# A low part's neighbour and a moved wait: two reorderings in a two-block fp32 layer on one core

## The reference, cut to what matters

```python
# first block
mod = silu(c) @ w_ada + b_ada          # 6 x 1024: shift, scale and gate, twice
h = rmsnorm(x) * (1 + sc_m) + sh_m
q, k, v, f, u = split(h @ w_in)        # 8 heads of 64, forget gates, 512 pooling columns
x = x + gt_m * (concat(attention(q, k, v, f), pool(u)) @ w_out)
h = rmsnorm(x) * (1 + sc_f) + sh_f
x = x + gt_f * moe(h)                  # 32 SwiGLU experts, top 2 of the best group of 8
# second block
x = x + hybrid(rmsnorm(x) @ w_in_2)    # stick-breaking attention and a gated recurrence
hn = rmsnorm(x)
x = x + square(relu(hn @ w_ff1)) @ w_ff2   # 1024 -> 4096 -> 1024
out = rmsnorm(x)
```

## Time and profile before

| | |
|---|---|
| median of 3 runs | 787.43 us |
| the profiled execution | 789.42 us |
| its span, first to last instruction | 787.6 us |
| mean granted clock of TensorE | 0.959 |
| PE busy | 705.3 us (90%) |
| DVE busy | 355.1 us (45%) |
| ACT busy | 301.4 us (38%) |
| DMA | 210.24 MB, mean 267 GB/s |

### The profile page before, as it was taken

The page is one execution under the profiler, slowest core; times in us unless marked ns, Lnnn a source line. Parts: engine busy times, 40 slices in busy tenths (PEclk is TensorE's granted clock), DMA queues, the critical chain, the costliest instruction groups (busy, mean ns, idle before and its releaser), DMA issues.

```text
span 787.6 us, 12575 instructions
## 1 busy us (share of the span) xinstructions
PE 705.3 (90%) x5226; PEld 543.6 (69%) x5226; DVE 355.1 (45%) x563; ACT 301.4 (38%) x444; POOL 46.5 (6%) x84
## 2 busy tenths in 40 slices
PE   4999899989876686667999999999998999999996
PEld 3787557964332232222898989898977999999995
DVE  2567742251101000102876677536575555555543
ACT  4344341042110110003676354678355534545432
POOL 0000000000000000000046650000000000000000
PEclk9999997999998887889999999999999999999999
DMA  8999599979999999999874523415344355544101
GB/s 337 413 416 363 216 377 406 421 287 423 420 424 422 424 421 424 420 419 415 317 263 157 209 109 114 167 42 214 107 155 175 126 214 214 214 167 166 43 1 53
DMA packets 33036, 210.24 MB, mean 267 GB/s; under 512 B 4688, under 2 KB 5072, under 8 KB 8656
## 3 DMA queue, kind: packets, MB, share of 16 engines
q1 hardware_dynamic: 32976, 209.38, 66.9%
HBM read 208.32 MB, written 1.05 MB: 266 GB/s over the span
## 4 chain that ended last, share of the span: by engine, by line
PE 68%; DMA 19%; DVE 7%; ACT 3%; issue 2%; SPq 1%; DVEq 0%; ACTq 0%
PE psum L419 67%; DMA raw<-in_w_exp 16%; DMA early<-in_w_ada_q 3%; DVE wlo L520 2%; PE psum L427 1%; ACT whi L495 1%; DVE acc L544 1%; SPq L474 1%; DVE XL L1978 0%; ACT Sp L846 0%; DVE XL L2372 0%; SPq L466 0%; DVE X L2414 0%; ACT G L1299 0%; DVE dT L1017 0%
## 5 line engine op out<-in xcount | busy, mean ns | idle before, releaser
L419 PE MATMUL psum<-XH,whi 128*128 128x256 f32 x736 | 211.8, 288 | 6.0 <-DVE XL L2372 3.1
L419 PE MATMUL psum<-XH,wlo 128*128 128x256 f32 x736 | 209.4, 285 | 0.0
L419 PE MATMUL psum<-XL,whi 128*128 128x256 f32 x736 | 209.3, 284 | 0.0
L520 DVE TENSOR_TENSOR wlo<-raw,whi 128x2048 fp32r<-128x2048 f32 (+1 forms) x88 | 169.0, 1959 | 48.6 <-ACT whi L495 48.6
L419 PEld LDWEIGHTS psum<-XH,whi 128*128 128x128 f32 x736 | 140.7, 191 | 10.6 <-DVE XL L2372 3.3
L495 ACT ACTIVATE whi<-raw 128x2048 fp32r<-128x2048 f32 (+1 forms) x79 | 139.3, 1801 | 22.5 <-PE psum L419 22.4
L419 PEld LDWEIGHTS psum<-XL,whi 128*128 128x128 f32 x736 | 140.3, 191 | 0.3
L419 PEld LDWEIGHTS psum<-XH,wlo 128*128 128x128 f32 x736 | 140.4, 191 | 0.0
L419 PE MATMUL psum<-raw,G 128*32 128x512 f32 x456 | 67.2, 676 | 18.9 <-DMA raw<-in_w_exp 18.8
L419 PE MATMUL psum<-raw,XT 128*32 128x512 f32 x248 | 37.6, 741 | 20.8 <-DMA raw<-in_w_exp 19.6
L419 PEld LDWEIGHTS psum<-raw,G 128*32 128x32 f32 x456 | 17.7, 122 | 55.4 <-issue 54.4
(11 more groups left out here) (349 smaller groups left out, 968.7 us busy)
## 6 DMA issues: line engine op xcount, KB each, us to landing
raw<-in_w_exp SPq DMA_DIRECT2D x85, 1024.0 KB, 24.2
raw<-in_w_ff SPq DMA_DIRECT2D x32, 1024.0 KB, 5.0
raw<-in_w_in SPq DMA_DIRECT2D x22, 1024.0 KB, 6.0
raw<-in_w_ada SPq DMA_DIRECT2D x16, 1024.0 KB, 10.2
raw<-in_w_in_t SPq DMA_DIRECT2D x8, 1024.0 KB, 17.2
X<-in_w_exp SPq DMA_DIRECT2D x5, 1024.0 KB, 25.0
raw<-in_w_ada_q SPq DMA_DIRECT2D x4, 1024.0 KB, 15.1
raw<-in_w_out_t SPq DMA_DIRECT2D x4, 1024.0 KB, 8.1
```

Source lines behind the costliest of these rows:

```text
L419: return e.matmul(o, l, r, start=start, stop=stop, skip_group_check=True)
L520: e.tensor_tensor(wlo[j % NS][:, x], ring[slot[i]][:, x], whi[j % NS][:, x], ALU.subtract).then_inc(*steps_(("lo", j, x.start // 1024), *[ ...
```

## The change

In DVE's list `dve_ada(e, 4)` moves from behind the low part of piece 20 and the maxima of heads 4 and 5 to just ahead of that low part. In PE's list the waits for the turned inputs' four banks move from ahead of the first projection's block 0 to between its block 1 and the first sum of the second projection. No instruction is added or taken out.

```diff
@@ dve_mixer
             dve_scale_probs(e, 2)
             dve_scale_probs(e, 3)
             dve_products(e, 5, 1)
+            dve_ada(e, 4)
             dve_pieces(e, 21)
             dve_scores(e, 4)
             dve_scores(e, 5)
-            dve_ada(e, 4)
             dve_probs(e, 2)
             dve_probs(e, 3)
             dve_ada(e, 5)
@@ pe_ff
-            for k in range(4):
-                if k in holder:
-                    e.wait_ge(*at(("read", holder[k])))
             banks = Banks([4, 5, 6, 7])
             for j in range(9):
                 if j < 8:
                     feature_major(e, banks, fj(1, j), "n4", ff_pe, ("ff1", j))
+                if j == 1:
+                    for k in range(4):
+                        if k in holder:
+                            e.wait_ge(*at(("read", holder[k])))
                 if j:
                     pe_ff2(e, banks, j - 1)
```

## The result

The changed kernel takes 781.35 us, the median of 8 runs (778.29 to 788.25); the kernel before, run beside it and counted with its first three, 786.51 us, the median of 8 (785.82 to 788.79). The ratio is 0.9929, with a 95% interval of 0.9906 to 0.9953: about 5.6 us or 0.7% faster. A second session gave 0.9927 (0.9903 to 0.9952). Of the 29 executions of the kernel before that the first four experiments are compared with, one of 794.96 us counts as slow: it is in their median, 787.68 us, and not in the ratios. The profiled execution took 783.02 us, with a span of 781.2 us.

The account below looks back on a forecast made before the run. Engines and DMA bound in turn up to about 170 us, the expert weights' DMA from 210 to 358 us, then PE. 3.80 + 2.15 = 5.95 us off 787.43 gave 781.5 us, range 779.5 to 783.5.

Parts of the forecast that it names:

- Both waits on the path: PE's 3.1 us wait for XL and 2.1 us wait for mcol both lie on the path that sets the end.
- The wait, 2.24 us: With `dve_ada(4)` earlier, the 12 matmuls behind `pe_probs(3)` start at 85.68 instead of 87.92: 2.24 us.
- The clock, 1.56 us: The 12 matmuls behind PE's wait stay at 2.4 GHz, taking 2.86 instead of 4.42 us: 1.56 us.
- clock not given back: Rival, chance 0.18: the 1.56 us come back as a slow stretch elsewhere in the mixer; gain 4.39, time 783.0.
- What is late next: `dve_ada(5)` at 89.53, low part of piece 22 at 90.92, SP's load of ada(9, 0) at 93.3: 3.8 us gained.
- Through the experts: The expert stream's restart waits for PE, so it comes 3.8 us earlier and the 3.8 us are passed on.
- experts absorb: Rival, chance 0.14: the first edit's gain is lost in 148 us of full DMA queue; gain 2.15, time 785.3.
- The second edit, 2.15 us: PE starts on the first XL slices at 599.43 instead of 601.80 and keeps step with DVE: 2.15 us.
- The sum: Both edits over the whole kernel: 3.80 + 2.15 = 5.95 us, from a median of 787.43 to 781.5; chance 0.50.
- The rule on the clock: The clock monitor runs freely, so the slow stretch behind PE's wait needn't be in every execution; sum then 2.24 + 2.15.

Follow-up runs that it names:

- the first four experiments: First edit alone, second edit alone, both again, and the kernel before with unread matmuls in PE's wait: 783.0, 783.41, 781.47 and 787.13 us.
- the filled wait: Kernel before plus 13 unread matmuls in PE's 2.1 us wait for line 579, between `pe_probs(2)` and `pe_probs(3)`: 787.13 us, ratio 1.0008.
- three gaps filled: Changed kernel plus unread matmuls ahead of PE's two 0.7 us waits for line 1020 and ahead of `pe_probs(7)`: 782.62 us, ratio 0.9921 to before.
- more gaps filled: Changed kernel plus unread matmuls ahead of two PE waits for line 1020, or also ahead of `pe_probs(7)`: 780.69 and 782.62 us.
- all slices awaited: Kernel before with the second edit plus a wait for the last pair of XL slices ahead of block 0: 789.11 us, ratio 1.0001.
- `dve_ada(4)` half the way: Kernel before with `dve_ada(4)` moved between the low part of piece 20 and the maxima of heads 4 and 5: 786.35 us, ratio 0.9974.

## Why the prediction was right

- **Both waits on the path.** Right: each edit alone moved the time, and the pieces that hold the waits are the ones that shrank.
- **The wait, 2.24 us.** Measured 3.85 (A-B, 16.05 to 12.20) less 1.54 for the clock: 2.31 us. The forecast took the matmuls behind it to start at 85.68; they did at 85.47, of which 0.14 lies ahead of A. `dve_ada(4)` ran at 83.94, 1.8 us after its input was ready.
- **The clock, 1.56 us.** 1.54 us, by the filled wait, in 3 of 3 profiled executions against 5 of 5. At this place the rival "clock not given back" falls. At the end of the kernel it doesn't: the timed runs with the wait filled show no gain, and the interval of the changed kernel, 3.7 to 7.4 us, holds the rival's 4.39 as well as the forecast's 5.95. Elsewhere the clock did take and give by chance: the granted clock over 85 to 140 us was 0.88 before, 0.91 changed and 1.00 in the changed kernel's second session.
- **What is late next.** 1.40 us from `dve_ada(5)` to the low part (89.32 to 90.72), against a forecast of 1.39, and SP's load followed (93.10; forecast 93.3).
- **Through the experts.** C-D is 423.6 to 424.4 us in 13 of the 14 executions of the table, whether the restart came at 165.9 or 174.5. In the one with three gaps filled it is 425.70, with the restart at 168.08; no run shows why. The rival "experts absorb" falls: the 210 to 358 us stream is full, but its start hangs on PE.
- **The second edit, 2.15 us.** 2.33 us on the spot. The term was short by 0.18 us, since I had taken the same 0.31 us to be paid at each start: the last six of the first 24 matmuls began 597.34 - 597.23 = 0.11 us after the last XL (which ends at 594.01 + 3.22). I also saw only one of the two ways in which this wait goes on. The profile of before had the clock at 1.00 there; of nine executions with the wait in place four had it fall, with D-E at 10.99 to 12.26 us instead of 9.60 to 9.63. Of five with the edit (7.22 to 7.27 us, the two with more gaps filled among them) none had. Over the nine the mean is 10.5 us, so the edit is worth 3.3 us on average by this count (an estimate), and the lower end of what its timed runs gave alone is 3.4. That the edit keeps the clock from falling is likely, not shown: five executions are few.
- **The sum.** 5.95 forecast; 6.4 between the two spans; 5.6 by the ratio, with 3.7 to 7.4 as its interval. The median of 781.35 against the 781.5 forecast is closer than the working deserves, and in part luck: the median of before was 787.43 in three runs, 786.51 in eight and 787.68 in the next session, and the edits alone gave 4.7 and 4.3 us where the terms are 3.80 and 2.15. That the terms are right is shown by the pieces of the profile, not by the medians.
- **The rule on the clock.** It says that the monitor isn't tied to the kernel's start (the Trainium skill, TensorE: Matmul & The Clock Gate, "Part 1: The HAM clock gate"). The traces fit it, without showing the reason: around the product of `w_out` the same program had a clock of 0.78 or 1.00 over 23 us. They don't bear out the step that I drew from it, that the fall behind the 2.1 us wait might often be absent.

Much of the spread of the runs goes with the clock too. Over 28 executions of the kernel before in one session the time goes with the mean granted clock with a correlation of -0.92, at 0.56 us for each 0.001; over the 8 of the changed one it is -0.96. In the other session's 24 executions of the kernel before it is -0.67, so the clock isn't all of it.

## What to carry to other kernels

A short wait of PE can cost itself and, behind it, the clock: here 2.1 us of standing still cost 3.85 on the spot, though the timed runs don't show the clock's share of it. So a tiny instruction that frees a buffer belongs ahead of the long ones on its engine as soon as its input is ready, and the work beside a slice-by-slice producer should wait for slices, not for the whole. A full DMA stream later in the kernel doesn't swallow such a gain when the stream's own start waits for the engine. And cut the executions at a few starts before believing a difference of medians: the piece that holds an edit repeats within 0.05 us as long as the clock in it is the same (A-B, D-E), where the whole scatters by 10. The other pieces need an eye: the start came up to 2.2 us late in three executions, and C-D was 1.3 us longer than in all others in one.

## What was not expected of the hardware

- Idleness of 2.1 us brought the clock from 2.4 to 1.2 GHz in 5 of 5 executions, 2.9 to 3.1 us of it at another place in 4 of 9, and 1.0 us in none of one. What PE did ahead of them differs: row products with 128x32 weights and one-column sums at the first, and 16 turns of 128 columns at the second.
- A slow stretch doesn't cost half its length, as the prediction took it to. In the kernel with all slices awaited the matmuls of 256 columns start 0.213 us apart at 1.2 GHz and 0.119 us apart at 2.4 GHz, so 28 of them in a slow stretch of 6 us lose 28 x 0.094 = 2.6 us (44%). In the kernel with `dve_ada(4)` half the way D-E shows 2.66 (12.26 - 9.60).
